# Narrow products in four column groups: index keys, head weights, delta gates and router of a two-block transformer kernel

## The reference, cut to what matters

```
layer 1 of the first block:   z, qkv, gate, b_raw, a_raw = split(rmsnorm(h) @ od_w_in)   # b_raw, a_raw: 4 columns each
                              beta = sigmoid(b_raw);  g = -exp(a_log) * softplus(a_raw + dt_bias)
second block, both layers:    k_idx = hn @ w[c_ki]  (32 columns);   w_idx = hn @ w[c_wi]  (8 columns)
                              score[t, s] = sum_h w_idx[t, h] * relu(q_idx[t, h] . k_idx[s]);  top 64 of s are kept
second block, last layer:     logits = hn @ router  (8 columns);  the two best experts of eight per token
```

## Time and profile before

| | us |
|---|---|
| median of 3 timed runs (all: 2664.25, 2668.19, 2664.0) | 2664.25 |
| the profiled execution, its own time | 2665.57 |
| its span, first to last instruction | 2663.8 |
| PE busy in the span | 2569.2 (96%) |
| DVE busy | 1674.3 (63%) |
| ACT busy | 1333.1 (50%) |
| POOL busy | 26.3 (1%) |

### The profile page before, as it was taken

One profiled execution on the slowest core, in us unless ns is written; L12 is line 12 of the kernel. 1 busy time (PEld: TensorE's weight loads), 2 busy tenths in 40 slices (PEclk: granted clock), 3 DMA queues, 4 the chain that ended last, 5 costly groups with the idle time before them and its releaser, 6 DMA issues.

```text
span 2663.8 us, 39895 instructions
## 1 busy us (share of the span) xinstructions
PE 2569.2 (96%) x14174; PEld 2117.6 (79%) x14174; DVE 1674.3 (63%) x2502; ACT 1333.1 (50%) x1966; POOL 26.3 (1%) x40
## 2 busy tenths in 40 slices
PE   7999999999999999998999998999999999999997
PEld 6676998887577997767998766888888888787886
DVE  1212776452116773645552646989898988989897
ACT  2212544411124443244332245777777777877785
POOL 0100000000000000000000000000000000000000
PEclk9999999999999999999999998999999999999999
DMA  8453644321536546215555215989898989889897
GB/s 325 159 189 121 243 189 186 134 95 64 221 111 245 189 189 242 100 64 221 189 189 184 96 64 210 381 326 378 318 376 329 372 336 368 334 344 358 334 367 278
DMA packets 87636, 627.33 MB, mean 236 GB/s; under 512 B 9760, under 2 KB 9920, under 8 KB 12800
## 3 DMA queue, kind: packets, MB, share of 16 engines
q1 hardware_dynamic: 84512, 613.45, 60.7%
q0 software_dynamic: 2480, 11.31, 1.1%
q10 hardware_dynamic: 560, 1.38, 0.1%
HBM read 625.06 MB, written 1.05 MB: 235 GB/s over the span
## 4 chain that ended last, share of the span: by engine, by line
PE 92%; DVE 3%; ACT 2%; DMA 1%; issue 1%; DVEq 0%; SPq 0%; ACTq 0%
PE bank L1020 23%; PE bank L909 13%; PE bank L606 12%; PE bank L1048 11%; PE bank L923 7%; PE bank L617 6%; PE bank L852 6%; PE bank L1131 1%; PE bank L1063 1%; PE bank L990 1%; PE bank L707 1%; PE bank L1035 1%; PE bank L687 1%; PE bank L673 1%; PE bank L638 1%
## 5 line engine op out<-in xcount | busy, mean ns | idle before, releaser
L1467 ACT ACTIVATE sb_parts<-sb_ring 128x1024 fp32r<-128x1024 f32 x873 | 872.9, 1053 | 86.1 <-PE bank L1048 38.8
L2245 DVE TENSOR_TENSOR sb_parts<-sb_ring,sb_parts 128x1024 fp32r<-128x1024 f32 x675 | 786.4, 1217 | 9.2 <-ACT sb_parts L1467 9.2
L1020 PE MATMUL bank<-sb_parts 128*128 128x512 f32 x2688 | 661.6, 396 | 2.5 <-DVE sb_parts L2237 1.8
L1020 PEld LDWEIGHTS bank<-sb_parts 128*128 128x128 f32 x2688 | 495.0, 188 | 113.4 <-issue 9.4
L909 PEld LDWEIGHTS bank<-sb_parts 128*128 128x128 f32 x3168 | 385.4, 193 | 9.8 <-issue 5.9
L909 PE MATMUL bank<-sb_parts 128*128 128x256 f32 x3168 | 387.1, 284 | 6.0 <-DVE sb_XT L2171 4.6
L1048 PE MATMUL bank<-sb_parts 128*128 128x512 f32 x1344 | 323.9, 390 | 0.0
L1048 PEld LDWEIGHTS bank<-sb_parts 128*128 128x128 f32 x1344 | 251.7, 188 | 52.1
L606 PE MATMUL bank<-sb_XT,sb_ring 128*128 128x256 f32 x1152 | 259.9, 386 | 8.0 <-DVE sb_XT L1996 4.6
L2148 DVE TENSOR_TENSOR sb_parts<-sb_ring,sb_parts 128x1024 fp32r<-128x1024 f32 x198 | 233.2, 1219 | 49.2 <-ACT sb_parts L1467 49.2
L606 PEld LDWEIGHTS bank<-sb_XT,sb_ring 128*128 128x128 f32 x1152 | 220.8, 193 | 43.4 <-issue 13.4
(11 more groups left out here) (345 smaller groups left out, 2077.6 us busy)
## 6 DMA issues: line engine op xcount, KB each, us to landing
sb_ring<-in_moe_panels SPq DMA_DIRECT2D x342, 1024.0 KB, 5.0
sb_ring<-in_ada_w SPq DMA_DIRECT2D x48, 1024.0 KB, 4.9
sb_ring<-in_ffn_w_up SPq DMA_DIRECT2D x44, 1024.0 KB, 6.2
sb_ring<-in_ffn_w SPq DMA_DIRECT2D x33, 1024.0 KB, 5.0
sb_ring<-in_w_in SPq DMA_DIRECT2D x26, 1024.0 KB, 4.9
sb_ring<-in_ffn_w_down SPq DMA_DIRECT2D x22, 1024.0 KB, 7.3
sb_ring<-in_xattn_wkv SPq DMA_DIRECT2D x16, 1024.0 KB, 4.8
sb_ring<-in_od_w_in SPq DMA_DIRECT2D x12, 1024.0 KB, 5.0
```

What stands on the lines that cost most here:

```text
L1020: m = nc.tensor.matmul(banks[par][:, :], x[:, k, :], w[:, cols], start=k == 0 and t == 0, stop=k == KD - 1 and t == 2, skip_group_check=True)
L1467: return nc.scalar.activation(out, in_, ACT.Copy)
L2245: V_.tensor_tensor(LOW[u], ring[slot][:, 1024 * c:1024 * c + 1024], HIGH[u], ALU.subtract) \
```

## The change

All four narrow products turn round: the narrow weight, 32 columns wide (8 real ones and 24 zeros for gates and router), is the stationary operand, XT moves with 256 columns, and chunk k goes to column group k mod 4 (`quarters`). ACT copies the result out, and a joining product with a matrix "quarter" (i mod 32 = j mod 32) sums the four groups (`joined`); for the index keys the same matrix, 128 wide, also puts the sum on all four groups. `fresh` waits for each tile of XT by itself in place of all four (`normed`).

With it: the panel of c_ki and c_wi is loaded and multiplied ahead of c_qi; GpSimd's copy and its semaphore go; in mix1 `take(4)` moves from behind the third qkv panel to between the parts and the joining product, and DVE's `taken(4)` ahead of its read of ba; WBA and WR become one tile WN, cleared by GpSimd, loaded with the gates' weights at the start and with the router's after layer 1's cross attention; the constants half0 and half1 shrink to one column, broadcast when used.

```diff
-IN_GROUPS = (("c_qi",), ("c_ki", "c_wi"), ("b_qd",), ...
+IN_GROUPS = (("c_ki", "c_wi"), ("c_qi",), ("b_qd",), ...
+    put("quarter", i % 32 == j % 32)
-        WK4 = r.tile(KD, 4 * 32)
+        KP = r.tile(2 * T)
+        SMALL = XHf[:, 0:T]
-        WBA = sb("WBA", KD, 8)
-        WR = sb("WR", KD, NE)
+        WN = sb("WN", KD, 32)
+            def quarters(ps, narrow, fresh=None):
+                for k in range(KD):
+                    g = 32 * (k % 4)
+                    if fresh and k % 2 == 0:
+                        wait_read(("norm", fresh, k // 2))
+                    m = nc.tensor.matmul(ps[g:g + 32, 0:T], narrow(k), XT[:, k, :], start=k < 4, stop=k >= 4,
+                                         skip_group_check=True)
+                return m
+            def joined(ps, src, at=0):
+                for tb in range(NT):
+                    m = nc.tensor.matmul(ps[:, at + tb * 8:at + tb * 8 + 8], src[:, tb * P:tb * P + P],
+                                         cst("quarter")[:, 0:8], start=True, stop=True)
+                return m
...
# PE, ffn3
-                normed("ffn3")
-                ps = claim("router")
                 pe.wait_ge(sem("router_loaded"), 16)
-                for tb in range(NT):
-                    for k in range(KD):
-                        m = nc.tensor.matmul(ps[:, tb * 8:tb * 8 + 8], XT[:, k, tb * P:tb * P + P], WR[:, k, :], ...
+                filled(quarters(claim("router_parts"), lambda k: WN[:, k, :], fresh="ffn3"), "router_parts")
+                wait_read("router_parts")
+                m = joined(claim("router"), SMALL)
# PE, mix1
-            normed("mix1")
-            ps = claim_aside("ba")
-            ... (16 matmuls of 8 columns)
+            filled(quarters(claim_aside("ba_parts"), lambda k: WN[:, k, :], fresh="mix1"), "ba_parts")
+            take(4)
+            wait_read("ba_parts")
+            m = joined(claim_aside("ba"), SMALL)
...
-                if j >= 2:
+                if j >= 3:
                     take(j + 2)
# PE, mix2 and mix3
+                pn, slot = panel()
+                wt = cols_of(slot)
+                ps = claim((k2, "c_kw"))
+                quarters(ps, lambda k: wt[:, k, 0:32], fresh=n)
+                filled(quarters(ps[:, T:2 * T], lambda k: wt[:, k, 32:64]), (k2, "c_kw"))
+                release(pn, (k2, "c_kw"))
                 panel_T((k2, "c_qi"))
-                ... (panel, wait for ki_spread, 8 matmuls with WK4, 16 matmuls of 8 columns, release)
+                wait_read((k2, "c_kw"))
                 ps = claim((k2, "c_ki"))
+                nc.tensor.matmul(ps[:, 0:T], cst("quarter"), KP[:, 0:T], start=True, stop=True)
+                filled(joined(ps, KP[:, T:2 * T], T), (k2, "c_ki"))
# ACT
+                evac("router_parts", SMALL, bank_of("router_parts")[:, 0:T])
+            evac("ba_parts", SMALL, bank_of("ba_parts")[:, 0:T])
+                evac((k2, "c_kw"), KP, bank_of((k2, "c_kw"))[:, :])
# DVE, mix1
+            taken(4)
             wait_full(dve, "ba")
...
-            taken(4)
             dve.wait_ge(sem("decay_maps"), 2)
# GpSimd
-            pool.dma_start(WBA[:, :, :], d["ba_w"]...)
-            pool.dma_start(WR[:, :, :], d["moe_router_2"]...)
+            step(G.memset(WN[:, :, :], 0.0))
+            pool.dma_start(WN[:, :, 0:8], d["ba_w"]...)
...
+            pool.dma_start(WN[:, :, 0:NE], d["moe_router_2"]...)   # after the sums of xat1
-                pool.wait_ge(landed[n % RING], 16 * (n // RING + 1))
-                G.tensor_copy(WK4..., ring[n % RING]...[:, :, :, 0:32].broadcast_to([P, KD, 4, 32]))
```

More of the change, by code:

```diff
@@ L56 @@
     _at += _w
-IN_GROUPS = (("c_qi",), ("c_ki", "c_wi"), ("b_qd",), ("b_kvd", "b_kr"), ("a_q",), ("a_k",), ("a_v",), ("d_q",),
+IN_GROUPS = (("c_ki", "c_wi"), ("c_qi",), ("b_qd",), ("b_kvd", "b_kr"), ("a_q",), ("a_k",), ("a_v",), ("d_q",),
                           ("d_k",), ("d_v",), ("c_q",), ("c_k",), ("c_v",))
@@ L72 @@
 CONST_AT, CONST_W = pack([("ident", P), ("causal", NT * T), ("chunked", NT * T), ("alibi", NT * HS * T),
-                          ("cum", P), ("same", P), ("half0", P), ("half1", P), ("strict", P),
+                          ("cum", P), ("same", P), ("half0", 1), ("half1", 1), ("strict", P),
                           ("strict_t", P), ("lev0", P)] + [(f"levt{i}", P) for i in range(len(LEVELS))]
-                         + [("upto", P), ("iota", P), ("cos", NT * 16), ("sin", NT * 16), ("eps", 1), ("ones", P)])
+                         + [("upto", P), ("iota", P), ("cos", NT * 16), ("sin", NT * 16), ("eps", 1), ("ones", P),
+                            ("quarter", P)])
 COL_AT, COL_W = pack([("mem_norm", KD), ("norm_mix", 2 * KD), ("norm_xattn", 2 * KD), ("norm_ffn", 2 * KD),
@@ L105, in shape_constants @@
     put("same", same)
-    put("half0", (i < C64) & (j >= 0))
-    put("half1", (i >= C64) & (j >= 0))
+    put("half0", i < C64)
+    put("half1", i >= C64)
     put("strict", same & (i > j))
@@ L326, in build_program @@
         moe_plan = {}
-        spread = {}
         block = ctx.enter_context(nc.Block())
@@ L953, in experts @@
             def experts():
-                normed("ffn3")
-                ps = claim("router")
                 pe.wait_ge(sem("router_loaded"), 16)
-                for tb in range(NT):
-                    for k in range(KD):
-                        m = nc.tensor.matmul(ps[:, tb * 8:tb * 8 + 8], XT[:, k, tb * P:tb * P + P], WR[:, k, :],
-                                             start=k == 0, stop=k == KD - 1)
+                filled(quarters(claim("router_parts"), lambda k: WN[:, k, :], fresh="ffn3"), "router_parts")
+                wait_read("router_parts")
+                m = joined(claim("router"), SMALL)
                 filled(m, "router")
@@ L1152, in _ @@
             for x, name in enumerate(("cum", "same", "half0", "half1")):
-                m = nc.tensor.matmul(ps[:, 8 * x:8 * x + 8], cst(name), sm("g", 8), start=True, stop=True)
+                m = nc.tensor.matmul(ps[:, 8 * x:8 * x + 8], cst(name).broadcast_to([P, P]) if x > 1 else cst(name),
+                                     sm("g", 8), start=True, stop=True)
             filled(m, "gsum")
@@ L1282, in _ @@
                 transpose_norm(n)
-                normed(n)
                 k2 = f"s{layer}"
@@ L1295, in index_scores @@
                                 filled(m, (k2, "idx", tb, j))
+                pn, slot = panel()
[4 more added lines that the diff above has]
+                release(pn, (k2, "c_kw"))
                 panel_T((k2, "c_qi"))
-                pn, slot = panel()
-                spread[layer] = pn
-                wt = cols_of(slot)
+                wait_read((k2, "c_kw"))
                 ps = claim((k2, "c_ki"))
[L1303 to L1311, removed]
+                nc.tensor.matmul(ps[:, 0:T], cst("quarter"), KP[:, 0:T], start=True, stop=True)
+                filled(joined(ps, KP[:, T:2 * T], T), (k2, "c_ki"))
                 take(14 + 6 * layer)
@@ L2745, in _ @@
             pool.dma_start(FN, d["final_norm"].broadcast_to([P, D])).then_inc(sem("final_gain_loaded"), 16)
+            pool.dma_start(WN[:, :, 0:NE], d["moe_router_2"].rearrange("p (k n) -> p k n", k=KD)) \
+                .then_inc(sem("router_loaded"), 16)
             wait_drained(pool, ("sum", "ffn1", 3))
```

8 lines of the change are left out of this document (1 added, 7 removed).

## The result

| | us |
|---|---|
| changed kernel, median of 4 runs (2634.23 to 2640.17) | 2636.98 |
| kernel before on the same chip, median of 4 runs | 2666.22 |
| ratio, 95% interval | 0.9885 [0.9874, 0.9897] |
| profiled execution of the changed kernel (its span) | 2637.37 (2635.6) |

The change makes the kernel faster, by 28 to 34 us of 2666. I had forecast 2642.5 with a range of 2639 to 2649: the direction was right and the gain too small, 22.4 where the two profiled executions differ by 28.2 (2665.57 to 2637.37).

The account below looks back on a forecast made before the run. PE's queue was taken to bound the kernel. Gains of 4.1 + 7.2 + 6.6 + 4.5 = 22.4 us gave 2643.2 from the profiled 2665.57, 2641.9 from the median; forecast 2642.5, range 2639 to 2649.

Parts of the forecast that it names:

- The bound, and that PE's time is the end's time: Whole kernel: PE busy 96% of the span, chain 92% PE, so a microsecond off PE's queue comes off the end.
- Prices: All four places: 57 ns a column-group pass plus 0.1 us per width change; full-width panel 6.91 us at full clock.
- Rival (b): All places: column groups do not overlap with these operands; 96 passes cost 216 ns each, 15 us, 2657.5; chance 0.05.
- the drain for a change of tiling: Four places, two drains each by the Trainium skill: 3.2 us off the gain at 0.4 each; taken as already inside 1.86.
- mix1: Delta stage's gates, up to gsum: shorter product, qkv panel at full clock, take(4) moved; gain 4.1 us, bounds 2.6 to 4.5.
- mix2: Index keys and head weights: gain 7.2 us, bounds 4.5 to 7.5, with c_qi 2.2 later by the order of loading.
- Rival (a): mix1, mix2, mix3: the clock falls all the same, price 6.0 us, 2648.5; chance 0.14.
- mix3: Same edit as mix2 with panels already landed: 23.5 us becomes 16.9, gain 6.6, bounds 4.8 to 7.0.
- Router: ffn3, up to the places: router ready 4.3 us earlier, gain 4.5 taken; DVE becomes the bound if the clock is up.
- What costs nothing: ACT's four copies, clearing WN, narrow loads in 1024 pieces and broadcast constants; 0 to 2 us allowed at ffn1, 0 taken.
- Rival (d): ffn1: the router's load in 1024 pieces clogs DMA queues and delays every panel, making the kernel slower; chance 0.03.
- Rival (c): Delta stage or router gives its gain back to DVE or ACT, about 4 us, 2646.5; chance 0.08.

Follow-up runs that it names:

- experiment 8: Changed kernel with panel c_qi first again, the key and head-weight parts behind it and the take over ACT's copy: 2640.39 us, ratio 0.9887.
- experiment 5: Changed kernel with index keys and head weights of mix2 and mix3 as before, bank turn held at the changed kernel's: 2653.2 us, ratio 0.9938.
- experiment 6: Changed kernel with mix1's delta gates as before, take(4) and taken(4) at their old places too: 2642.75 us, ratio 0.9899.
- experiment 2: Changed kernel with the old bank turn at ffn2, three banks skipped ahead and one behind: 2637.97 us, ratio 0.9896.
- experiment 7: Changed kernel with the router at ffn3 as before, 32 passes of 8 columns, XT stationary: 2641.1 us, ratio 0.9892.
- experiments 1: Kernel before with only the changed kernel's bank turn at ffn2, one bank skipped ahead and three behind: 2662.14 against 2666.12 us, ratio 0.9988.

## Why the prediction was right in direction and too small in size

- **The bound, and that PE's time is the end's time**: right. PE's chain share stayed 92%, and the gains of the stages (28.0) are in the end time (28.2 in this pair of profiles, 29.2 and 32.4 by the two pairs of medians).
- **Prices.** Column groups at about 57 ns a pass: x32 took 1.93 us behind c_qi in experiment 8, whose weights are the ring's; with its waits for tiles 2.38 to 2.51. Rival (b), no overlap, fell. So did the drain for a change of tiling: experiment 8's x32 is 1.86 us from its start to the next full-width start, exactly, and c_qi ahead of it takes 8.76 from start to start, where experiment 5's, with no change of width behind it, takes 8.67.
- **mix1**, 4.1 forecast, 4.5 measured (experiment 6: 5.8 in the end time). The join is at 467.24 where I had about 467.3, but this stage began 0.5 us later than in the kernel before, so it came 0.6 sooner than worked out. My step that the parts wait for the bank of the first modulation sum was wrong: their first pass starts at 464.76 and ACT's first copy of those sums at 465.22. The parts ran tile by tile and had ended at 466.34, 0.6 sooner than I had them, so the waiting tile by tile did buy something. Gates were ready before gsum.
- **mix2**, 7.2 forecast, 7.4 measured. The order of loading cost what I said (c_qi starts 5.96 us behind the first turning matmul, 3.90 before), and the clock stayed up behind it. Rival (a) fell: b_qd and the qkv panel are at 7.15.
- **mix3**, 6.6 forecast, 7.8 measured. 1.5 of it is the 16 turning matmuls ahead of the stage's first edit, 3.44 us at L638 before and 1.94 after; I took the work up to XT as unchanged. That difference belongs to the moment at which the clock falls, not to an edit: experiment 5, with the old mixers, has 1.94 there too, and experiment 2, with the new ones, 3.53.
- **Router**, 4.5 forecast, 5.4 measured at the places. The logits were there 0.6 us sooner than I had them (5.33 us after the first turning matmul; my 1616.9 is 5.9 after 1610.99), and the choice then set the end. Some of it was lost again before the expert loop; the end time says 4.1 (experiment 7).
- **What costs nothing**: right. Rival (d) fell: the router's load landed 5.5 us after issue, the gates' 20.7, and the number of DMA packets is the same as before (87636), so the 1024 pieces that I counted do not show as packets. Rival (c) holds for the router only, as a wait of 1.71 us inside the gain.
- **The step that failed** is the sum itself. It let only the four changed places change, and took every stage between them as it was. The step "mix2" counts the removed and added passes, but not that one bank more is claimed and the turn of the banks moves on by one. That has its consequence in the next stage, ffn2, which gained 2.9 us: 1.6 by the earlier start (experiments 1 and 2) and 1.3 by the clock behind it, which moves from profile to profile. My range's lower end was built from the four stages' upper bounds (they sum to 24.0, where I wrote 25), with no term for untouched stages, and so was too narrow on that side: ffn2's 2.9, mix3's 1.2 and the router's 0.9 make 5.0 of the missing 5.8, mix1 0.4. This holds for the first pair of profiles; the second profile of the changed kernel is 7 us shorter with the same stages, so the stretches between them can move the end by as much as the whole miss, and the first median stood only 2 us outside the range.

## What to carry to other kernels

Where PSUM banks are handed out in turn, one claim more changes which tile shares a bank with a later product: write down the order of banks at every stage behind the edit, and look in the profile before for a matmul that starts exactly as the reader of its bank's last contents ends. A narrow product is worth turning round twice over, for its own passes (57 ns in a column group against 4.44 / 32 = 0.14 us for 8 moving columns with a full stationary operand) and for the dense work behind it; it also fills the rest before its operand is complete, tile by tile. For the range, give stretches that the diff does not touch a term of their own, of the size by which profiles of kernels with the same code there differ: 1 to 2 us here for most of them, and 7.5 for the one from gsum to the next stage (225.65 to 233.12 us).

## What the runs showed of the hardware that I had not expected

- The clock falls behind narrow passes with PE busy throughout: with 32 passes of 8 columns put back, the dense panel behind took 8.53 and 8.60 instead of 7.15 us. The Trainium skill, "TensorE: Matmul & The Clock Gate", section "Why this matters for your kernels", gives as its practical rule to leave no long idle gaps of PE; here PE was not idle in that stretch, so that rule alone would have forecast 7.15, and the rows decide.
- The same instructions behind the same rest took 7.15 or 8.83 us, by what clock was granted in them (experiment 8). Likewise at the start of ffn1, which the change does not touch, the 16 turning matmuls of the kernel before and then of the changed one:

```profile
816.26 1.94 PE L638 MATMUL bank<-sb_CST,sb_XH 128*128 128x128 f32 x16 [1.62 <-DVE sb_XH L1981]
```

```profile
810.44 3.34 PE L656 MATMUL bank<-sb_CST,sb_XH 128*128 128x128 f32 x16 [1.94 <-DVE sb_XH L1993]
```

The rests ahead of them are 1.62 and 1.94 us, so nearly but not wholly the same. There the changed kernel lost 1.4 us, in a stage without an edit.
